# First modulation columns of a DiT block's kernel fetched in two halves, and the first product block split to match

## What is computed

```
mod_l = (jax.nn.silu(c) @ w_ada[l] + b_ada[l]).reshape(B, N_MOD, 1, D)
mod_c = (jax.nn.silu(c_ctx) @ w_ada[l] + b_ada[l]).reshape(N_MOD, 1, 1, D)
...
def _modulate(x, shift, scale):
    return x * (1.0 + scale) + shift

def _swiglu(h, w13, w2):
    a = h @ w13
    return (jax.nn.silu(a[..., :D_FF]) * a[..., D_FF:]) @ w2
```

## Time and profile before

| what | value |
|---|---|
| median of 3 runs | 2186.39 us (2184.72 to 2191.35) |
| profiled execution, its own time | 2185.09 us |
| its span in the profile | 2183.3 us |
| PE busy | 98% of the span |
| DVE, ACT busy | 70%, 41% |
| granted TensorE clock, mean | 0.996 |

### The profile page before, as it was taken

The page is one execution under the profiler, slowest core; times in us unless marked ns, Lnnn a source line. Parts: engine busy times, 40 slices in busy tenths (PEclk is TensorE's granted clock), DMA queues, the critical chain, the costliest instruction groups (busy, mean ns, idle before and its releaser), DMA issues.

```text
span 2183.3 us, 32181 instructions
## 1 busy us (share of the span) xinstructions
PE 2147.8 (98%) x11775; PEld 1830.7 (84%) x11779; DVE 1518.7 (70%) x2595; ACT 889.6 (41%) x1502; POOL 160.8 (7%) x201
## 2 busy tenths in 40 slices
PE   9999999999999999999999999999999999999998
PEld 7888888888888888899789878888778888888886
DVE  5788887777557976755752356765767777767787
ACT  3622222222246545532544337743523233326444
POOL 0000000000000010360000004611000000000001
PEclk9999999999999999999999999999999999999999
DMA  8154444555278665532330003342143434438773
GB/s 291 32 162 149 141 135 145 161 165 174 78 254 293 216 185 171 157 124 61 106 102 21 20 1 106 108 135 77 55 139 120 149 124 128 142 129 310 274 232 115
DMA packets 261843, 310.41 MB, mean 142 GB/s; under 512 B 19350, under 2 KB 164686, under 8 KB 261710
## 3 DMA queue, kind: packets, MB, share of 16 engines
q1 hardware_dynamic: 250670, 300.13, 43.0%
q10 hardware_dynamic: 11040, 8.52, 1.3%
HBM read 242.13 MB, written 66.45 MB: 141 GB/s over the span
## 4 chain that ended last, share of the span: by engine, by line
PE 87%; DVE 7%; ACT 3%; issue 2%; DMA 1%; SPq 0%; POOL 0%; ACTq 0%; DVEq 0%; POOLq 0%
PE psum L1293 11%; PE psum L1294 11%; PE psum L1295 11%; PE psum L1493 6%; PE psum L1495 6%; PE psum L1494 6%; PE psum L1998 2%; PE psum L2000 2%; PE psum L1999 2%; PE psum L2419 2%; PE psum L1313 2%; PE psum L1312 2%; PE psum L1311 2%; PE psum L2973 1%; PE psum L2402 1%
## 5 line engine op out<-in xcount | busy, mean ns | idle before, releaser
L1293 PE MATMUL psum<-x_mix_h,x_op_h 128*128 128x512 f32 x640 | 251.1, 392 | 4.2 <-DVE v_sum L1100 4.0
L1294 PE MATMUL psum<-x_mix_l,x_op_h 128*128 128x512 f32 x640 | 249.5, 390 | 0.0
L1295 PE MATMUL psum<-x_mix_h,x_op_l 128*128 128x512 f32 x640 | 249.3, 389 | 0.0
L1495 PE MATMUL psum<-s_high,s_low 128*128 128x512 f32 x616 | 239.7, 389 | 0.0
L1494 PE MATMUL psum<-s_low,s_high 128*128 128x512 f32 x616 | 239.7, 389 | 0.0
L1493 PE MATMUL psum<-s_high 128*128 128x512 f32 x616 | 239.6, 389 | 0.0
L1480 DVE TENSOR_TENSOR s_low<-s_raw,s_high 128x1024 fp32r<-128x1024 f32 x154 | 186.9, 1218 | 51.0 <-ACT s_high L1441 51.0
L1441 ACT ACTIVATE s_high<-s_raw 128x1024 fp32r<-128x1024 f32 x154 | 161.2, 1057 | 124.3 <-PE psum L1495 56.3
L985 ACT ACTIVATE x_op_h<-raw 128x512 fp32r<-128x512 f32 x140 | 86.0, 627 | 208.9 <-PE psum L1295 128.8
L985 ACT ACTIVATE x_op_h<-w_sum 128x512 fp32r<-128x512 f32 x160 | 97.0, 625 | 164.1 <-DVE w_sum L963 108.7
L1293 PEld LDWEIGHTS psum<-x_mix_h,x_op_h 128*128 128x128 f32 x640 | 120.3, 188 | 29.0 <-DVE x_op_l L991 2.9
(11 more groups left out here) (405 smaller groups left out, 5142.9 us busy)
## 6 DMA issues: line engine op xcount, KB each, us to landing
raw<-in_ffn_w SPq DMA_DIRECT2D x88, 512.0 KB, 5.5
f_terms<-g_half SPq DMA_DIRECT2D x154, 256.0 KB, 2.3
s_raw<-f_terms SPq DMA_DIRECT2D x154, 256.0 KB, 3.3
s_raw<-in_ffn_w SPq DMA_DIRECT2D x154, 256.0 KB, 4.1
ada_slice<-in_w_ada SPq DMA_DIRECT2D x112, 256.0 KB, 3.0
c_raw<-in_ffn_w SPq DMA_DIRECT2D x22, 512.0 KB, 3.8
p_raw<-in_w_in SPq DMA_DIRECT2D x22, 512.0 KB, 5.0
early<-in_w_ada SPq DMA_DIRECT2D x16, 512.0 KB, 6.4
```

Source lines behind the costliest of these rows:

```text
L1293: nc.tensor.matmul(o, wh[:, k], high(k), start=i < 4 and k == 0, stop=False, skip_group_check=i > 3)
L1294: nc.tensor.matmul(o, wh[:, k], low(k), start=False, stop=False, skip_group_check=i > 3)
L1295: last = nc.tensor.matmul(o, wl[:, k], high(k), start=False, stop=k == KH - 1, skip_group_check=i > 3)
L1495: return nc.tensor.matmul(o, l[:, 0, rows], h[:, 1], start=False, stop=i == PAIRS - 1, skip_group_check=True)
```

## The change

The sixteen pieces are cut another way: a piece now holds 128 rows of `w_ada` by 512 shift columns and the 512 scale columns that belong to them (two runs of 2 KB for each partition, before one of 4 KB). Pieces 0 to 7 are columns 0 to 511 of both vectors, pieces 8 to 15 columns 512 to 1023. SP issues pieces 0 to 7, the four row tiles, the two weight pieces, then pieces 8 to 15. DVE sums each half apart, and the context's sums of the second half come last. The first block's products for `k` 0 to 3 run on PE ahead of most of the second half's shift matmuls; those for `k` 4 to 7 come after them. The first rows are scaled directly from PSUM, as those of the second chunk are, and the copy in SBUF is gone. The context's scale is summed on PE in one piece inside the second item.

```
         def early_load(sp, i):
...
-            at = D * (1 - i % 2)
-            sp.dma_start(early[i][:], ada_view[:, i // 2, at:at + D]).then_inc(early_in[i % 4], 16)
+            columns = ada_view[:, i % KD, 0:2 * D].rearrange("p (s h c) -> p s h c", s=2, h=2)[:, :, i // KD, :]
+            sp.dma_start(early[i][:], columns).then_inc(early_in[i % 4], 16)
...
+        def early_shift_pe(pe, h, k):
+
+            i = KD * h + k
+            wait_early(pe, i)
+            for n in range(KH):
+                m = KH * h + n
+                nc.tensor.matmul(psum[:, 7, 2 * m:2 * m + 2], early[i][:, 0, n * P:(n + 1) * P], more_c[:, k, :],
+                                 start=h == 0 and k == 0 and n == 0, stop=k == KD - 1, skip_group_check=True)
...
+        def early_scale_ctx_pe(pe):
+
+            pe.wait_ge(mod_ready, 1)
+            pe.wait_ge(early_dve, scales_made(1, KD - 1, 1))
             for n in range(KD):
...
         def first_pe(pe, rows_wait):
 
-            beside = (10, 4, 12, 3, 4, 17, 6, 4)
             for k in range(KD):
-                idle_pe(pe, beside[k])
-                early_shift_pe(pe, k)
-                if k == 1:
+                idle_pe(pe, 1 if k else 7)
+                early_shift_pe(pe, 0, k)
+                if k == 3:
                     pe.wait_ge(bias_in, 3 * 16)
                     nc.tensor.transpose(psum[:, 0, 0:120], rows_a[0:120, :], ident[0:120, 0:120]).then_inc(rows_turned, 1)
-                if k == 2:
-                    idle_pe(pe, 8)
-                    turn_pe(pe, T1, T1_BANKS, rows_wait, 0)
             early_scale_pe(pe, 0)
-            idle_pe(pe, 10)
-            pe.wait_ge(F1.lo, 2)
-            for k in range(KD):
+            idle_pe(pe, 8)
+            for k in range(KH):
+                turn_pe(pe, T1, T1_BANKS, rows_wait, (0, k))
+            idle_pe(pe, 6)
+            for part in range(2):
+                pe.wait_ge(F1.lo, part + 1)
+                for k in range(KH):
+                    pe.wait_ge(T1.low, k + 1)
+                    plain_step(pe, F1, 0, part, k)
+                    if k % 2:
+                        turn_pe(pe, T1, T1_BANKS, rows_wait, (0, KH + 2 * part + k // 2))
+                    if part and k % 2:
+                        if k == 1:
+                            pe.wait_ge(early_dve, scales_made("known"))
+                        early_shift_pe(pe, 1, k // 2)
+            for k in range(2, KD):
+                idle_pe(pe, 1)
+                early_shift_pe(pe, 1, k)
+            early_scale_pe(pe, 1)
+            idle_pe(pe, 6)
+            for k in range(KH, KD):
                 pe.wait_ge(T1.low, k + 1)
                 for part in range(2):
                     last = plain_step(pe, F1, 0, part, k)
-                if k == 0:
-                    early_scale_pe(pe, 1)
             last.then_inc(F1.ab_ready, 1)
-            pe.wait_ge(mod_ready, 2)
...
-            for k in range(KD):
-                first_turned_act(act, k)
-            first_high(act, F1)
-            act.wait_ge(T1.scaled, KD)
+            act.wait_ge(early_dve, scales_made("known"))
+            half_act(act, F1, T1, T1_BANKS, 0, range(1))
+            first_high(act, F1, 0)
+            half_act(act, F1, T1, T1_BANKS, 0, range(1, 2))
+            first_high(act, F1, 1)
+            half_act(act, F1, T1, T1_BANKS, 0, range(2, KH))
             act.wait_ge(mod_ready, 1)
-            for k in range(KD):
-                first_scaled_act(act, k)
-            second_block_high(act, F1)
+            half_act(act, F1, T1, T1_BANKS, 0, range(KH, KH + 2))
+            second_block_high(act, F1, 0)
+            half_act(act, F1, T1, T1_BANKS, 0, range(KH + 2, KD))
+            second_block_high(act, F1, 1)
             silu(act, F1, 0)
```

More of the change, by code:

```diff
@@ L662, in early_shift_pe @@
-        def early_shift_pe(pe, k):
-            wait_early(pe, 2 * k + 1)
-            for n in range(KD):
[L666 to L675, removed]
-            last.then_inc(early_used, 1)
@@ L678, in early_known_dve @@
[L678 to L702, removed]
+        def early_scale_dve(dve, h, k, v):
+            i = KD * h + k
+            wait_early(dve, i)
+            factor = more[:, v * KD + k:v * KD + k + 1]
+            sums = early_sums[:, v, h * BANK:(h + 1) * BANK]
+            if k:
+                dve.wait_ge(early_dve, scales_made(h, k - 1, v))
+                nc.vector.scalar_tensor_tensor(sums, early[i][:, 1], factor, sums, op0=ALU.mult, op1=ALU.add)\
+                    .then_inc(early_dve, 1)
+            else:
+                nc.vector.tensor_scalar_mul(sums, early[i][:, 1], factor).then_inc(early_dve, 1)
@@ new lines, in early_shift_pe, with early_scale_pe @@
+        def early_shift_pe(pe, h, k):
+            i = KD * h + k
+            wait_early(pe, i)
[3 more added lines that the diff above has]
+                                 start=h == 0 and k == 0 and n == 0, stop=k == KD - 1, skip_group_check=True)
+        def early_scale_pe(pe, h):
+            pe.wait_ge(early_dve, scales_made(h, KD - 1, 0))
+            for n in range(KH * h, KH * h + KH):
+                last = nc.tensor.matmul(psum[:, 7, 2 * KD + n:2 * KD + n + 1], early_sums[:, 0, n * P:(n + 1) * P], ones[:],
+                                        start=False, stop=True, skip_group_check=True)
+            last.then_inc(early_used, 1)
@@ L704, in hybrid_block, with early_known_ctx_dve @@
+        def early_known_ctx_dve(dve):
+            dve.wait_ge(early_used, 3)
+            nc.vector.tensor_tensor(in_scale[:, 1], psum[:, 7, 3 * KD:4 * KD], early_bias[:, 0], ALU.add).then_inc(mod_ready, 1)
         MODS_LATE = N_MOD - 2
@@ L3102, in output_act @@
                 norm_act(act, N2, t, t)
-            first_high(act, F2)
+            for i in range(2):
+                first_high(act, F2, i)
             norm_act(act, N2, 4, 4)
@@ L3143, in output_dve @@
                 if (half, t) == (1, 3):
-                    first_low(dve, F2)
+                    for i in range(2):
+                        first_low(dve, F2, i)
                 if (half, t) == (1, 5):
@@ L3477, in _ @@
             half_act(act, F2, T3, T3_BANKS, 1, range(KD))
-            second_block_high(act, F2)
+            for i in range(2):
+                second_block_high(act, F2, i)
             silu(act, F2, 0)
@@ L3497, in _ @@
             dve.wait_ge(rows_kept, 1)
-            for k in range(KD):
-                early_scale_dve(dve, k)
-                if k == 2:
+            for k, v in [which[1:] for which in SCALE_ORDER[:2 * KD]]:
+                early_scale_dve(dve, 0, k, v)
+                if (k, v) == (4, 1):
                     dve.wait_ge(rows_turned, 2)
@@ L3544, in _ @@
             half_dve(dve, F2, T3, 1, range(KD))
-            second_block_low(dve, F2)
+            for i in range(2):
+                second_block_low(dve, F2, i)
             glu(dve, F2, 0)
```

98 lines of the change are left out of this document (56 added, 42 removed).

## The result

| 20 runs of each on one chip | median us | lowest to highest |
|---|---|---|
| before | 2188.55 | 2182.15 to 2191.35 |
| changed | 2193.07 | 2187.75 to 2199.30 |

What follows compares the result with a forecast made beforehand. PE, busy 98% of the span, was taken to bound the kernel. Full-clock gain -4.5 plus 1.7 moved scale gives -2.8; clock falls add 2.8 and 1.7: +1.7 on the 2186.39 median, 2188.1 us, range 2180 to 2194.

Steps and rivals of the forecast that it cites:

- The clock: PE's thin filler in the head and again from 36 to 43 us drops the clock: +2.8 and +1.7 us.
- What bounds the kernel now: PE is busy 98% of the span; early changes pay only by PE arriving sooner; first block ends at 57.96 before.
- Loads: Column pieces 1.3 us each, weight pieces 2.5; eighth piece lands at 15.2, row tiles 20.4, last piece 35.8.
- Rival 4: Rows of 2 KB load more slowly than 4 KB: +0.4 on the forecast, 2186 to 2189; chance 0.10.
- What stands behind them: Six pieces queued on PE behind the first 24 products, 6.3 us; at full clock the block ends 53.5, 4.5 earlier.
- Added behind: Context scale matmuls move into the second item, +1.7 us; DVE's wait for them costs nothing.
- The clock, head: Clock falls after the fourth or fifth piece, first product near 28: +2.8 us, lower 0, upper +5.7.
- The clock, second stretch: A pair or two of the late pieces and the scale at half rate: +1.7 us, range 0 to +7.
- The sum: -2.8 + 2.8 + 1.7 = +1.7 us; first block ends about 58.0 as before, the moved scale stays as a loss.
- 1 (the clock holds): Clock stays full in both stretches: -2.8 us, 2183.6; chance 0.22.
- 2: Second half follows its load, not PE's order: -9 us, 2177.4; chance 0.10, with what lies halfway.
- 3 (slower): Clock falls early in the head and stays down through the scale and second stretch: +8 us, 2194.4; chance 0.11.

Runs made afterwards that it cites:

- e1: Changed kernel with three fillers instead of one ahead of each piece of the first half; ratio against before 1.0011.
- e2: Changed kernel with six of the second half's shift pieces beside the first 24 products, not behind them; ratio against before 0.9996.
- i2: Changed kernel, unaltered, profiled a second time; 2189.69 us, last turn of the second item at 76.28.
- j2: Changed kernel, unaltered, profiled a third time; 2194.87 us, last turn of the second item at 79.20.
- j4: Changed kernel, unaltered, profiled a fourth time; 2200.14 us, last turn of the second item at 81.65.
- i1: Changed kernel with e1's edit and two fillers instead of one ahead of each of the six late pieces; ratio against before 0.9995.
- h1: Kernel before with eight fillers instead of four ahead of its last shift piece; ratio against before 1.0009.
- g1: e3 with the context's sums made earlier on DVE and the context scale back in the first block; 2184.68 us, ratio against before 0.9985.
- i3: g1's kernel profiled a second time, one run; 2187.78 us, last turn of the second item at 69.12.
- g3: Edits of g1 and g2 together; 2181.38 us, ratio against before 0.9971.
- e3: Changed kernel with both edits, e1's and e2's; ratio against before 0.9985.
- g2: e3 with three fillers instead of one ahead of each of the last two shift pieces; 2183.58 us, ratio against before 0.9983.
- i4: Kernel before, unaltered, profiled a second time; last turn of the second item at 75.84.
- j1: Kernel before, unaltered, profiled a third time; last turn of the second item at 75.84.
- j3: Kernel before, unaltered, profiled a fourth time; 2188.68 us, last turn of the second item at 72.44.
- e4: Changed kernel without the six late pieces of the second half's shift and their fillers (output lacks them); ratio against before 0.9971.

## Why the prediction failed, step by step

The step that failed is **The clock**: its two terms, +2.8 for the head and +1.7 for the second stretch, were too small. Against the sum's own figures for the full clock, the head came 4.4 late and the stretch 1.9 in the profiled execution, 5.5 and 3.3 in the mean of four. Of this 2.1 is offset because the head of before also falls in two of four, which the base of the sum left out. The mechanism, two falls at these two places, was right. A second, smaller step was wrong too: the loads, which would have kept the first product 1.6 us later than said even with the clock whole.

- **What bounds the kernel now.** Right that the first 70 us pay only by PE's arrival. But 57.96 was the end of one execution, with a last turn at 72.0 where two of four have 75.8. "The sum +1.7 is a difference, so it goes on the median" took the head of this execution for that of all.
- **Loads.** "I take 1.3" a piece: they came 1.4 apart, and the eighth landed at 15.9 (15.2 said). In e1 the four row tiles were there at 22.2, not 20.4, and with the clock whole the first product is at 26.7, not 25.1: the -2.8 of the full-clock sum was 1.6 too good in the head. In the changed kernel this is hidden, since PE comes to the turns 3 us after 22.2. Rival 4 is not shown: 1.4 a piece is also what the earlier trace rows gives for before (2.75 for two).
- **What stands behind them.** Right, and the largest lever of all: e2 took 4.6 us off at the last turn.
- **Added behind.** Right in both parts: 1.7 for the context scale, nothing for DVE's wait.
- **The clock, head.** "If it falls after the fourth or fifth piece, three or four pairs lose 0.8 each": it fell within the fourth; four pairs, the scale and all eight fillers ran at half rate. The text has the four turns end "near 24.7-25"; they began at 25.22. Its own terms for four pairs and eight slow fillers give 26 (15.2 + 0.84 + 4 x 0.8 + 0.84 + 0.84 + 3.4 + 1.75). The first product came at 29.46, 4.4 after the 25.1 of the full clock, where +2.8 was said (27.9). Against e1, whose clock was whole, it is 2.8, and 3.9 in the mean of four; e1's head is itself 1.6 later than the sum had it, by the row tiles. It was also a case taken for a value: in i2, j2 and j4 the first product is at 28.76, 31.06 and 33.02, as the fall lasts to 27.9 in j2 and the clock was never up in j4. The mean of the four is 30.6, which is +5.5; the "upper +5.7" was no tail, two of four lie beyond it.
- **The clock, second stretch.** "+1.7": from 40.71 to 47.94 the six pairs took 7.2 instead of 6.2, and the scale 1.72 instead of 0.84: 1.9 in the profiled execution. In i2, j2 and j4 the fall came one or two pieces earlier, and pairs and scale took 10.2, 10.9 and 11.3 instead of 7.1: 3.1, 3.8 and 4.3.
- **The sum.** In the profiled execution it missed by 1.94 us at the end of the first block (59.90, not 57.96), 1.6 of them in the head (29.46, not 27.9). At the last turn +1.7 was forecast, +3.7 was measured in the first pair of executions and +4.2 in the mean of four. Signs and places were right, the size too small.
- **Rivals.** 1 (the clock holds) was seen in no execution of the changed kernel. 2 exists, but needs the order of e2. 3 (slower) named the right mechanism and place, and 2194.4 is nearer to 2193.07 than the forecast is; it had 0.11. Part of that nearness is luck: it is built on a base of 2186.39 that came out 2.2 low, and its +8 is more than the 5.5 measured.
- **"A difference that arises after 120 us"** was listed as what would make the prediction wrong: there may be one. The means of four differ by 2.1 us behind the last turn, with the `v_sum` wait at 130 in it, against a spread of 5 to 6 within a kernel.

## What to carry to other kernels

Where PE runs small matmuls between loads, the time of a stretch can be a draw between two rates, as here; read several executions before a trace's microseconds are taken as the base of a sum, and price the half rate as a likely case, not as the tail (here six of six heads with single fillers). An early start of products is worth nothing if the work that releases the rest of the block is queued behind them: interleave it (e2), then look at the fillers. Count a clock's fall by its durations, not by the clock row alone.

## What the hardware did that was not expected

- The clock fell with PE busy for all of the time, on matmuls of one or two columns with some filler between them (at 11.4 and 45.5 in the changed kernel, 37.9 in before, 43.3 in i1 under two fillers a piece); in h1 it fell at 26.7 and stayed down for about eight fillers in a row.
- In every profile the first four fillers, from 2.1 us on, take 1.89 or about 0.43 each: each execution starts at half rate. It rose between about 6 and 9 us in all but j4 (about 29) and g1's first (about 36).
- The granted clock reads 1.00 up to its first recorded change, also where seven fillers take 3.17 and a piece 1.71 (j4; g1 likewise). Mean clocks of such executions are too high: g1's is 0.999, with the latest last turn but one (79.44).
- Behind PE's wait for `v_sum`, of 2.6 to 3.5 us in nine executions (the changed kernel, i1, i2, i3, j2, j4, e2, g3, h1), the clock fell in all but i2; where it was 1.7 to 2.3 (before, e1, e3, g1, g2, i4, j1, j3) in none, though e4's fell near it at 1.8.
